# Hybrid decoder step on one core: page loop over two PSUM banks, row-tiled sample states, last product by token ranges

## The reference

```python
# samples attend to 1024 paged tokens: compressed blocks, selected blocks, a window of 512
ck = rms_norm(compress_block(cmp_rows[:, :, :, 0], phi_k_w1, phi_k_w2), k_cmp_g)
cv = compress_block(cmp_rows[:, :, :, 1], phi_v_w1, phi_v_w2)
s_s = jnp.einsum('bqgrd,bgqnjd->bgrqnj', qc, k_g) * SCALE + b_s
s_w = jnp.einsum('bqgrd,bkgd->bgrqk', qc, w_rows[:, :, 0]) * SCALE
# recurrence, one token of a sample: state S is 128 x 128 for each of 4 heads
S = jnp.exp(b_last)[..., None] * S + jnp.einsum('bshk,bshv->bhkv', kc * jnp.exp(b_last[:, None] - b), vc)
o = jnp.einsum('bthk,bhkv->bthv', qc * jnp.exp(b), S)
# feed-forward, D_FF = 2816 = 22 tiles of 128, output 1024 = 8 channel tiles of 128
ext = jnp.concatenate([conv_state.astype(xn2.dtype), xn2 @ w_gate], axis=1)
c = conv_b + sum(conv_w[j] * ext[:, j:j + L] for j in range(CONV_W))
x = x + (jax.nn.silu(c) * (xn2 @ w_up)) @ w_down
return x, new_kv, new_win_state, S_new, ext[:, -(CONV_W - 1):]
```

## Time and profile before

| | |
|---|---|
| median of 3 runs | 2083.81 us (2081.81 to 2091.86) |
| the profiled execution's own time | 2082.97 us |
| its span, first to last instruction | 2081.3 us |
| mean granted TensorE clock | 0.961 |
| TensorE busy | 1952.8 us (94%) |
| VectorE, ScalarE, GpSimd busy | 878.3, 583.2, 155.2 us |

### The profile page before, as it was taken

How to read it: one execution, slowest core, us unless ns; L and a number is a source line. 1 busy time by engine, 2 the same in 40 slices (tenths; PEclk the granted TensorE clock), 3 DMA queues, 4 the chain that set the end, 5 groups by cost and what they waited for, 6 DMA issues and landing times. The chain is left out here.

```text
span 2081.3 us, 38167 instructions
## 1 busy us (share of the span) xinstructions
PE 1952.8 (94%) x15620; PEld 1762.3 (85%) x15620; DVE 878.3 (42%) x1690; ACT 583.2 (28%) x1192; POOL 155.2 (7%) x214
## 2 busy tenths in 40 slices
PE   5899979999986899879999999999999999999997
PEld 4668756676663889769999999999999999999997
DVE  6233025666613276623223334644244424442454
ACT  5133135666502134322212222221111111121121
POOL 4000001100030142410000000000000000000000
PEclk8899958999998899998999999999999999999999
DMA  7431544000065311123221122111111111111112
GB/s 237 67 68 61 224 122 120 9 2 2 2 213 215 104 34 35 44 57 99 76 77 48 36 82 82 51 40 41 51 50 50 38 53 41 50 38 53 51 30 94
DMA packets 164842, 148.15 MB, mean 71 GB/s; under 512 B 7746, under 2 KB 152083, under 8 KB 163651
## 3 DMA queue, kind: packets, MB, share of 16 engines
q1 hardware_dynamic: 153636, 124.82, 20.0%
q0 software_dynamic: 6208, 17.67, 3.4%
q10 hardware_dynamic: 4864, 3.79, 0.7%
HBM read 120.54 MB, written 29.99 MB: 72 GB/s over the span
## 5 line engine op out<-in xcount | busy, mean ns | idle before, releaser
L247 PE MATMUL psum<-xgl,t_wh 128*128 128x344 f32 x1056 | 338.2, 320 | 0.0
L246 PE MATMUL psum<-xgh,t_wh 128*128 128x344 f32 x1056 | 338.0, 320 | 0.0
L248 PE MATMUL psum<-xgh,t_wl 128*128 128x344 f32 x1056 | 337.3, 319 | 0.0
L247 PEld LDWEIGHTS psum<-xgl,t_wh 128*128 128x128 f32 x1056 | 198.6, 188 | 0.1
L248 PEld LDWEIGHTS psum<-xgh,t_wl 128*128 128x128 f32 x1056 | 198.4, 188 | 0.0
L246 PEld LDWEIGHTS psum<-xgh,t_wh 128*128 128x128 f32 x1056 | 198.2, 188 | 0.1
L248 PE MATMUL psum<-hh,t_wl 128*128 128x344 f32 x528 | 169.0, 320 | 0.0
L246 PE MATMUL psum<-hh,t_wh 128*128 128x344 f32 x528 | 168.9, 320 | 0.0
L247 PE MATMUL psum<-hl,t_wh 128*128 128x344 f32 x528 | 168.8, 320 | 0.0
L466 ACT ACTIVATE t_wh<-t_raw 128x1024 fp32r<-128x1024 f32 x75 | 79.2, 1056 | 206.0 <-PE psum L248 206.0
L518 DVE TENSOR_TENSOR t_wl<-t_raw,t_wh 128x1024 fp32r<-128x1024 f32 x100 | 122.0, 1220 | 34.3 <-ACT t_wh L466 29.2
(11 more groups left out here) (430 smaller groups left out, 3815.7 us busy)
## 6 DMA issues: line engine op xcount, KB each, us to landing
t_raw<-in_w_gate SPq DMA_DIRECT2D x22, 512.0 KB, 3.8
t_raw<-in_w_up SPq DMA_DIRECT2D x22, 512.0 KB, 3.8
t_raw<-in_w_down SPq DMA_DIRECT2D x24, 384.0 KB, 3.5
cmp_pages<-in_cache_kv SPq DMA_DIRECT2D x64, 128.0 KB, 2.2
t_raw<-in_w_in SPq DMA_DIRECT2D x16, 512.0 KB, 4.2
raw_n<-in_w_in SPq DMA_DIRECT2D x24, 256.0 KB, 3.7
r_raw<-in_w_in SPq DMA_DIRECT2D x12, 512.0 KB, 4.0
xh_copy<-xh SPq DMA_DIRECT2D x1, 4128.0 KB, 13.0
```

The lines of the kernel that those rows point to most:

```text
L246: pe.matmul(out, wh, xh, start=(first and k == 0), stop=False)
L247: pe.matmul(out, wh, xl, start=False, stop=False)
L248: mm = pe.matmul(out, wl, xh, start=False, stop=(last and k == n - 1))
```

## The change

**Page loop.** All 128 `compress` units now stand ahead of the loop. The turns are numbered q = 3 s + x and go alternately to bank 7 (even q, copied by ACT) and bank 3 (odd q, copied by DVE); turn q waits for the copy of turn q - 2, and turn 1 for the gelu, whose input lies in banks 0 to 3. The second product, the norm and its matmul are placed between the turns. The window's loads for samples 2 to 7 move from ACT's queue to SP's, and the way back of `xh` and `xl` waits for `s_ckt` in place of the last compress, since the norm's scratch now lies in their place.

**Samples in the mixer.** The samples' keys and values lie at partitions 32 h to 32 h + 7 for head h. One transpose in place of four turns the keys. POOL writes one 128 x 1024 `r_vm` in slot 10 in place of four of 8 x 1024. `sample_outer` runs twice, with two heads each, on 32 rows of the array per head; `sample_read` runs twice, with the query repeated over 32 columns as weights and the state moving, in four column groups. The sums then lie across partitions, so ACT and DVE copy them and PE turns them back (`turn_read`, 8 transposes).

**Last down product.** It is taken out of the loops and runs by token ranges 0 to 384, 384 to 768 and 768 to 1032, with 4 banks in turn, and keeps all 8 weight tiles (`down_high`, `down_low`). The gate columns are transposed during the first range and copied by ACT; each range's tiles of `y` are transposed, copied and stored during the next. `store_y` and its block are gone.

```diff
@@ finish, PE
-                with pe.Fori(0, KD // 2) as i:
-                    for b in range(2):
-                        down(i * 2 + (units[g] + 2 * n + b), b, i + (h0 + n), g, n)
-    store_y(c, io, tail, m_at)
+    RANGES = ((0, 384), (384, 768), (768, NT))
+            for r, (a, b) in enumerate(RANGES):
+                for ch in range(KD):
+                    n = KD * r + ch
+                    if r == 0:
+                        pe.wait_ge(raw_free, UL + ch + 3)
+                    if n >= 4:
+                        pe.wait_ge(dn_free, n - 3)
+                    else:
+                        pe.wait_ge(bank_free[0], UL // 2 - BASE + 1)
+                        pe.wait_ge(bank_free[1], UL // 2 - BASE + 1)
+                    for k in range(NL):
+                        if n == 0:
+                            pe.wait_ge(h_ready, KF - NL + k + 1)
+                        mm = three_pass(pe, c.psum[:, n % 4, 0:b - a],
...
+                    if r == 0 and ch >= 2:
+                        turn_tail(ch - 2)
+                    if r and ch >= 2:
+                        turn_y(turns[r - 1][(ch - 2) // 2], ch % 2)
+            pe.wait_ge(dn_free, 3 * KD)
+            for tt in turns[2]:
+                turn_y(tt, 0)
+                turn_y(tt, 1)
@@ finish, DVE
+                    if r == 0 and ch + 1 < KD:
+                        last_low(ch + 1)
+                    dve.wait_ge(dn, n + 1)
+                    dve.tensor_tensor(x2[:, ch, a:b], x2[:, ch, a:b], c.psum[:, n % 4, 0:b - a], ALU.add).then_inc(dn_free, 1)
+                    if r and ch in (3, 5, 7):
+                        store(turns[r - 1][(ch - 3) // 2])
@@ recurrent_mixer, PE
-                    mm = pe.matmul(c.psum[:, X + 2 * ((h + 1) % 2) + j, :], k8[:, h * P:(h + 1) * P], vm[h % 2][:, j * 512:(j + 1) * 512],
+                    for h in (h0, h0 + 1):
+                        r32 = slice(32 * h, 32 * h + 32)
+                        mm = pe.matmul(c.psum[:, X + 2 * ((h + 1) % 2) + j, :], k8[r32, :], vm[r32, j * 512:(j + 1) * 512],
...
-                    mm = pe.matmul(c.psum[:, O, h * NS + s:h * NS + s + 1], ss[h][:, s * P:(s + 1) * P], q8[:, h, s:s + 1], start=True, stop=True)
+                        mm = pe.matmul(c.psum[g0:g0 + 32, O + h0 // 2, at0:at0 + P], q8[:, h, s:s + 1].to_broadcast([P, 32]),
+                                       ss[h][:, s * P:(s + 1) * P], start=True, stop=True)
...
-                if 47 <= j < 51:
-                    sample_outer(j - 47)
-                if 51 <= j < 55:
-                    sample_read(j - 51)
-                if j == 56:
+                if j in (47, 50):
+                    sample_outer(0 if j == 47 else 2)
+                if j in (51, 54):
+                    sample_read(0 if j == 51 else 2)
+                if j in (55, 56):
+                    turn_read(j - 55)
+                if j == 57:
                     sample_sums()
@@ attend_samples, PE
-            compress(0, 80)
-            for s in range(NS):
-                x = 80 + 6 * s
-                turn(s, 0)
-                compress(x, x + 2)
-                turn(s, 1)
-                compress(x + 2, x + 4)
-                turn_window(s)
-                compress(x + 4, x + 6)
-                if s % 2:
-                    score(s - 1)
+            compress(0, 2 * HD)
+            for q in range(3 * NS):
+                turn(q)
+                if q == 2:
...
+                if q == 6:
...
+                if q % 6 == 5:
+                    score(q // 3 - 1)
```

More of the change, by code:

```diff
@@ L324, in finish @@
     prod = [c.sem(f"f_prod{i}") for i in range(2)]
+    w_up = [c.sem(f"tw_up{i}") for i in range(2)]
+    dn, dn_free, yt, ev_a, ev_v, tail_t, tail_s, tail_out = (
+        c.sem(x) for x in ("dn", "dn_free", "yt", "yev_a", "yev_v", "tail_t", "tail_s", "tail_out"))
+    out = [c.sem(f"y_out{i}") for i in range(3)]
     win, st_in, st_t, st_s = c.sem("win_out"), c.sem("st_in"), c.sem("st_t"), c.sem("st_s")
@@ L338, in finish @@
     BASE = NM // 2
+    NL = FF_GROUPS[GEND]
+    UL = units[GEND] + 2 * NL
+    RANGES = ((0, 384), (384, 768), (768, NT))
+    turns = [[0, 1, 2], [3, 4, 5], [6, 7, 8]]
     cols = lambda t: slice(t * TC, (t + 1) * TC)
@@ L501, in _, with last_high, tail_rows, store @@
                         down_turn(i, False)
-                else:
-                    with act.Fori(0, KD // 2 - 1) as i:
-                        down_turn(i, False)
-                    down_turn(KD // 2 - 1, True)
+            def last_high(d):
+                u = UL + d
+                upper = (d // 2) % 2
+                if upper:
+                    act.wait_ge(w_up[d % 2], 16 * (d // 4 + 1))
+                else:
+                    act.wait_ge(w_in[d % 2], 16 * (UL // 2 + 1 + d // 4))
+                act.wait_ge(prod[1 if d >= 2 else d], UL // 2 - BASE + 1)
+                act.activation(last(wh, dh, d), raw[:, d % 2, 4 * upper:4 * upper + NL, :], ACT.Copy).then_inc(hi, 1)
+            def tail_rows(j):
+                act.wait_ge(tail_t, j + 1)
+                w = min(4, KF - 4 * j) * P
+                act.activation(rows_out[:, 4 * j * P:4 * j * P + w], c.psum[0:10, 4 + j % 4, 0:w], ACT.Copy).then_inc(tail_s, 1)
+            def store(tt):
+                n = rows(tt)
+                if tt >= 3:
+                    act.wait_ge(out[tt % 3], 16 * (tt // 3))
+                act.wait_ge(yt, 2 * tt + 1)
+                act.activation(ys[0:n, tt % 3, 0:512], c.psum[0:n, 4 + 2 * (tt % 2), :], ACT.Copy).then_inc(ev_a, 1)
+            for d in range(1, KD):
+                last_high(d)
+                if d >= 4:
+                    tail_rows(d - 4)
+            tail_rows(4)
+            tail_rows(5)
+            for tt in range(NTT):
+                store(tt)
         @block.vector
@@ new lines, in _, with turn_tail @@
+                if g < GEND:
+                    with pe.Fori(0, KD // 2) as i:
+                        for b in range(2):
+                            down(i * 2 + (units[g] + 2 * n + b), b, i + (h0 + n), g, n)
+                    pe.sem_inc(h_free, 1)
+            def turn_tail(j):
+                if j >= 4:
+                    pe.wait_ge(tail_s, j - 3)
+                else:
+                    pe.wait_ge(tail_d, KF)
+                for k in range(4 * j, min(4 * j + 4, KF)):
+                    mm = pe.transpose(c.psum[0:10, 4 + j % 4, (k % 4) * P:(k % 4 + 1) * P], tail[:, k, :], c.ident[:, :])
+                mm.then_inc(tail_t, 1)
@@ L2267, in attend_samples @@
     NB = NS * 32
-    TB = 7
     ckt = c.low("s_ckt", [P, NB])
```

381 lines of the change are left out of this document (199 added, 182 removed).

## The result

| | before | after |
|---|---|---|
| median | 2087.84 us (4 runs, 2081.81 to 2096.21) | 2065.64 us (4 runs, 2064.16 to 2067.46) |
| profiled execution, own time | 2082.97 us | 2064.16 us |
| its span | 2081.3 us | 2062.5 us |

A forecast was written before the change was run, and what follows sets the result against it. TensorE, busy for 1952.8 of 2081.3 us, was taken to bound the kernel. Page loop -0.3, mixer -8.0 and last product and output -2.6 sum to -10.9 us from a median of 2083.81: 2072.9 us, range 2069 to 2078.

The forecast's parts named there:

- Mixer, forecast -8.0: Samples in the mixer's last slots: outer products, reads and the work ahead of them together save 8.0 us.
- the stretch at a low clock behind it stays too: Mixer, behind TensorE's 3.06 us wait for `logged`: matmuls still start 0.29 us apart, at 1.2 GHz.
- Outer products: Mixer: two calls of 1.95 us replace four of 1.98, if row groups overlap; gain 4.0 to 3.8 us.
- Reads: Mixer: 64 passes at 0.042 us plus two transpose groups at 0.59 replace four calls; gain 3.3 to 3.6 us.
- Ahead of it: Mixer, before the outer products: fewer key transposes and earlier DVE states save TensorE 0.5 us.
- Last product, forecast -2.6: Last down product and output: less work behind the products, partly returned as transposes and waits; net 2.6 us saved.
- the price of 0.59 us for four transposes: Last product: 12 turns of `x2b` among the products cost 12 x 0.59 = 7.1 us at most.
- Page loop, forecast -0.3: Samples' page loop: the second bank's gain is spent on lost compress cover; only the chain behind the loop is saved, 0.3 us.
- The rival that a score runs at the low clock: Page loop: part of the 0.27 rival of clock falls in new gaps, 2074.4 to 2077.4 us in all.
- Row groups do overlap: Mixer: the rival, chance 0.15, said they do not; outer calls stay 7.8 us, total 2076.8 us.
- the page loop did not run at the low clock as a whole: Page loop: the slower rival, chance 0.08, had low clock throughout, 2097 us, or from half on, 2085.4.
- The clock rival: Last product and page loop: new waits start 1.2 GHz stretches costing 1.5 to 4.5 us; chance 0.27.

The follow-up runs named there:

- lower group: The 40 of 94 executions of the unchanged kernel before that took under 2088.5 us; their median is 2082.3 us.
- the three sets with the unedited change: Three follow-up sets, each on a chip of its own, that ran the change unedited beside the kernel before; its 15 runs have a median of 2065.6 us.
- upper group: The 54 of 94 executions of the unchanged kernel before that took above 2088.5 us; their median is 2094.1 us.
- the second and third profiles of the change: Later profiled executions of the change, repeated without edits; the repeats measured 2066.31 us and 2064.86 us.

## Why the prediction was wrong

**What "before" is.** The forecast was summed against a profiled execution of the lower group and carried to a median of three runs, 2081.81, 2083.81 and 2091.86, as if they were one spread. They were two groups. The change's own lower-group gain, 2082.3 to 2065.6, is 16.7 us; against the medians of before in the three sets with the unedited change it is 22 to 28. Between the profiles 18.8 us went where 10.9 were forecast: 3.7 more in the last product, 2.1 more in the mixer, 0.2 between them, 3.5 ahead of all edits, and 1.6 less ahead of the mixer.

**Mixer, forecast -8.0, measured -10.1 in the profiles.** The step that failed is "the stretch at a low clock behind it stays too". It went: 3.0 us at 0.58 and 4 us at 0.88 cost 3.0 x 0.42 + 4 x 0.12 = 1.7 us that the profile after doesn't pay; the second and third profiles of the change pay some of it (0.66 over 895 to 900, 0.72 over 900 to 905). In the upper group it cost 12 us more, and there the change takes it in more than half of all executions. The experiments show the cause on both sides: without the wait, or with the mixer of the change, the upper group is gone, and with the old reads put back the low stretch is back. What puts one execution of before in the upper and another in the lower group is not shown. *Outer products* -3.9 forecast, 17.80 to 13.58 us between the first call and the wait, -4.2. *Reads* -3.5 forecast: before 4 x 1.71 = 6.8 us (910.88 to the next half-tile at 912.59), after 2 x 1.01 and 0.9 for the two groups of transposes at 0.46, 2.9: -3.9. The 0.042 us a pass from the earlier trace rows was too dear, 64 passes took 2.0 us. *Ahead of it* -0.5 forecast, -0.2 measured (187.94 to 187.70): `r_y` sums of head 3 did fall to 0.29 us, but TensorE then waited 0.49 for DVE's states. The mask in slot 10 made DVE's sums of head 0 1.3 us later, as forecast without effect on TensorE.

**Last product, forecast -2.6, measured -6.3.** The step that failed is the price of 0.59 us for four transposes among products, taken from the page loop. From 2011.60 to 2014.12 are 2.52 us for 12 matmuls at 0.172 and four transposes (each leaves one record): 0.46. A row of before's own last stage would have given it, 8.05 us for 72:

```profile
2059.69 8.05 PE L771 MATMUL psum<-ident,x2b 128*128 128x128 f32 x72 [1.59 <-PEq L343]
```

The 17.5 groups at 0.46 are 8.0 against 10.3. The products took 0.172 and 0.120 a matmul for 384 and 264 columns, 44.5 in place of 45.4 us; the waits 1.68 and 0.44, 2.1 in place of 2.5. Together they are 54.7 of the 55.2 us up to 2055.3. The forecast had 58.2 for this at 0.59 a group and 57.0 at 0.5, and took the middle, 57.6. The end behind that, 7.2 us for 8.3, went by the chain forecast, tile 8 waiting for tile 5's store.

**Page loop, forecast -0.3, measured -0.3** to the next block's L2476 / L2564, and the equal number is in part luck. To that block's first matmul it is 77.7 us before (578.06 to 655.76) and 78.5 after (574.59 to 653.05), 0.8 more, with one score at half rate in it. From there to L2476 / L2564 it is 4.9 and 3.8, at a granted clock of 0.50 and 0.74. Then come +1.6 ahead of the mixer that the forecast didn't have, at a mean granted clock of 0.60 against 0.66; why it is lower there is not shown (busy times of the five engines, then clock, DMA share, GB/s; after, then before):

```profile
656.86:690.91 34.05, 14.94 (x235) 12.70 (x235) 10.64 (x33) 6.96 (x15) 1.25 (x3) 0.60 0.50 159
```

```profile
660.67:693.11 32.44, 13.30 (x236) 11.70 (x236) 10.65 (x33) 7.04 (x15) 0.96 (x1) 0.66 0.60 200
```

The rival that a score runs at the low clock came true once (3.52 us) and cost 1.6 (3.52 - 1.91), inside the 82.27.

**Rivals.** Row groups do overlap, and the page loop did not run at the low clock as a whole. The clock rival looked only for new falls; the old one was the large term. No rival held a time under 2070, and none asked what the low stretch depends on. The factor of up to 4 of the Trainium skill (TensorEngine Tiling (Array Packing), where it stands in section Overview, Theoretical Speedup) would have given 2070.0 by the prediction's estimate; the reads went from 4 x 1.71 to 2 x 1.01 us, 3.4 times, the outer products from 4 calls to 2 of the same length, 2.0 times, which agrees with two row groups in use. The 2.5 that the prediction read from the trace's forms is 2.7 (1.84 / 16 = 0.115 against 0.042).

**Ahead of the samples,** -3.5 us with no edit. At 62 us the two profiles are 0.5 us apart, at 82 us 3.2, and TensorE's granted clock differs over 50 to 100 us of the span (TensorE busy, clock), before and after:

```profile
50.00:100.00 50.00, 41.78 (x171) 0.80 0.43 73
```

```profile
50.00:100.00 50.00, 42.02 (x184) 0.86 0.46 75
```

Compress starts at 576.9 to 578.1 in the six profiles of before and its forms with one edit, and at 574.6 to 580.5 in the twelve of the change and its forms. The means are 577.6 and 576.8, so most of the 3.5 us is the luck of which execution was profiled. It doesn't save the range: the run of the change nearest its median, 2065.55 us, has compress at 576.2; with 577.6 it would take 2067.0 (an estimate), still under 2069. What sets this start in an execution is open.

## What to carry to other kernels

When three runs of one kernel differ by 0.5%, find the stage that differs before pricing a change: profile it again until both groups are seen. A stretch at a low clock is not a constant that moves with its wait; look at which matmuls run in it. Here it lasted some 25 us with one-column reads in it and at most some 6 us with the reads in a wide form, and an earlier release of the wait kept it from starting. Price a small group of matmuls from its neighbours in its own stage.

## What the hardware showed that was not expected

- After an idle time of 3.06 us TensorE stayed at 1.2 GHz for some 25 us while its records show it busy without a gap, half-tiles of 344 columns and single-column reads in turn. In the profiles with the same wait and the reads in their wide form the low stretch was 0 to about 6 us.
- Two heads of single-column reads in a row (32 records, 3.6 us) brought the clock from 2.4 to 1.2 GHz with no idle time directly ahead of them.
- Four matmuls of 512 columns on two row groups take 1.99 us in either order, and the reads of two heads 1.01 us with neighbours in different column groups and 1.05 with neighbours in the same one.
